# A top-4 mixture-of-experts layer: expert work in 32-token groups on four column tiles, with VectorE turning the rows

## The reference

```python
logits = xt @ w_router + b_router                 # 1024 tokens, 32 experts
top_val, top_idx = lax.top_k(logits, 4)
top_w = softmax(top_val)
...
gate = xblk @ w_gate[e] + b_gate[e]               # per expert, over its tokens
up = xblk @ w_up[e] + b_up[e]
gate = minimum(gate, 7.0); up = clip(up, -7.0, 7.0)
h = (up + 1.0) * gate * sigmoid(1.702 * gate)
y_expert = h @ w_down[e] + b_down[e]
...
y = sum over a token's four experts of top_w * y_expert
out = x + gt2 * rms_norm(y, g_post_ffn)
```

## Time and profile before

| | us |
|---|---|
| median of three runs | 2531.75 |
| the profiled execution, first to last instruction (span) | 2541.4 |
| TensorE busy in it | 2373.6 (93%) |
| VectorE, ScalarE, GpSimd busy | 723.2, 498.1, 421.2 |
| TensorE on the chain that ended last | 88% |
| DMA, mean over the span | 231 GB/s |

### The profile page before, as it was taken

The page is one execution under the profiler, slowest core; times in us unless marked ns, Lnnn a source line. Parts: engine busy times, 40 slices in busy tenths (PEclk is TensorE's granted clock), DMA queues, the critical chain, the costliest instruction groups (busy, mean ns, idle before and its releaser), DMA issues.

```text
span 2541.4 us, 31972 instructions
## 1 busy us (share of the span) xinstructions
PE 2373.6 (93%) x11147; PEld 1211.2 (48%) x11148; DVE 723.2 (28%) x1243; ACT 498.1 (20%) x1116; POOL 421.2 (17%) x528
## 2 busy tenths in 40 slices
PE   5999999998987699999999999999999999999992
PEld 3575756775553354444444444344444444444430
DVE  4155565363466110111111111111111111111114
ACT  5122212233452010111111111111111111111112
POOL 5000000003003631111121111211111111111112
PEclk9999999998986799999999999999999999999996
DMA  8112110136024586677789989889888998999985
GB/s 281 33 34 75 33 46 30 58 99 229 34 93 167 208 283 210 197 269 243 271 298 374 334 293 370 311 311 359 326 277 278 316 330 298 375 328 341 325 310 201
DMA packets 216274, 587.81 MB, mean 231 GB/s; under 512 B 21338, under 2 KB 81266, under 8 KB 216210
## 3 DMA queue, kind: packets, MB, share of 16 engines
q1 hardware_dynamic: 131650, 337.94, 36.1%
q10 hardware_dynamic: 55504, 197.22, 20.7%
q0 software_dynamic: 29056, 51.75, 9.5%
HBM read 548.46 MB, written 38.37 MB: 231 GB/s over the span
## 4 chain that ended last, share of the span: by engine, by line
PE 88%; DVE 4%; issue 2%; DMA 2%; ACT 1%; POOL 1%; ACTq 0%; SPq 0%; DVEq 0%; POOLq 0%
PE ps L1900 25%; PE ps L1927 14%; PE ps L1959 12%; PE ps L1973 7%; PE ps L1656 5%; PE ps L1757 4%; PE ps L1652 4%; PE ps L1662 2%; PE ps L1713 2%; PE ps L1659 2%; PE ps L1938 2%; PE ps L1863 2%; DMA w_up_e<-in_w_up_dram 1%; PE ps L1895 1%; PE ps L1735 1%
## 5 line engine op out<-in xcount | busy, mean ns | idle before, releaser
L1900 PE MATMUL ps<-w_up_e,xT 128*128 128x512 f32 x736 | 345.9, 592 | 0.0
L1900 PE MATMUL ps<-w_gate_e,xT 128*128 128x512 f32 x736 | 345.9, 592 | 0.0
L1959 PE MATMUL ps<-w_down_e,hT 128*128 128x512 f32 x736 | 319.7, 592 | 0.0
L1475 DVE TENSOR_SCALAR oh_gu<-part_e,tab_e 128x128 bf16<-128x128 f32 x48 | 13.8, 287 | 992.2 <-PE ps L1900 598.9
L1030 ACT ACTIVATE sig_sb<-gate_sb 128x1024 f32<-128x1024 f32 x47 | 49.7, 1058 | 1074.4 <-DVE gate_sb L1481 1074.4
L1927 PE MATMUL ps<-w_gate_e,xT 128*32 128x256 f32 (+1 forms) x1504 | 228.4, 473 | 4.2 <-DMA w_up_e<-in_w_up_dram 4.2
L1927 PE MATMUL ps<-w_up_e,xT 128*32 128x256 f32 (+1 forms) x1504 | 227.2, 470 | 0.0
L1900 PEld LDWEIGHTS ps<-w_up_e,xT 128*128 128x128 f32 x736 | 139.8, 190 | 176.0 <-issue 176.0
L1900 PEld LDWEIGHTS ps<-w_gate_e,xT 128*128 128x128 f32 x736 | 139.9, 190 | 168.5 <-issue 165.3
L1959 PEld LDWEIGHTS ps<-w_down_e,hT 128*128 128x128 f32 x736 | 138.0, 190 | 165.0 <-issue 165.0
L1973 PE MATMUL ps<-w_down_e,hT 128*32 128x256 f32 (+1 forms) x1504 | 191.8, 478 | 7.9 <-issue 7.9
(11 more groups left out here) (384 smaller groups left out, 2363.9 us busy)
## 6 DMA issues: line engine op xcount, KB each, us to landing
w_down_e<-in_w_down_dram ACTq DMA_DIRECT2D x368, 512.0 KB, 4.6
w_gate_e<-in_w_gate_dram SPq DMA_DIRECT2D x256, 512.0 KB
w_up_e<-in_w_up_dram SPq DMA_DIRECT2D x256, 512.0 KB
w_ring<-in_w_ada_dram SPq DMA_DIRECT2D x17, 1024.0 KB, 5.2
w_ring<-in_w_in_dram SPq DMA_DIRECT2D x20, 512.0 KB, 5.2
w_first<-in_w_ada_dram SPq DMA_DIRECT2D x7, 1024.0 KB, 12.4
x_all<-in_x_dram SPq DMA_DIRECT2D x2, 2048.0 KB, 10.5
w_out<-in_w_out_dram SPq DMA_DIRECT2D x8, 512.0 KB, 8.6
```

The costliest lines, as they stand in the source:

```text
L1900: last = T.matmul(ps[:, b, :], xT[:, k, :], wgt[b // 2][:, k, (b % 2) * 512:(b % 2) * 512 + 512], start=False, stop=k == KT - 1)
L1959: last = T.matmul(ps[:, 4 + b, :], hT[:, k, :], wgt[2][:, k, b * 512:b * 512 + 512], start=k == 0, stop=k == KT - 1)
```

## The change

The routing, the expert loop and its data layout are rewritten; the mixer is the same.

- **TensorE.** An item is cut into 1 to 4 groups of 32 tokens. For each k-slice and group, four matmuls run on the four column tiles of the array: 32 tokens stand still, tile j streams its quarter of the weight columns, 512 columns for gate and up together, 256 for down. The `rows` and `hidden` transposes, the bias matmuls and `slot_sums` are gone. An item's form is now its number of groups, chosen by nested `If`/`Else`; one register load (`item_pair`) brings the forms of both items and the expert.
- **VectorE.** It turns the gathered rows (`rows_turned`), turns gate and up out of PSUM in 32x32 blocks, adds the bias to the turned values, clamps, multiplies, and writes `hT` directly.
- **GpSimd.** Rows move in quarters (1 KB) so that a group's rows land on four sets of 32 partitions: four gathers and four adding scatters for an item. Each scatter waits until the one before it has landed. `idx_g` and `idx_s` are worked out per item from `slot_tab`.
- **Slots.** A token's slot is (position in its expert, expert) alone, so VectorE's `place(t)` and GpSimd's `put_slots(t)` run tile by tile beside the routing; SyncE reads the finished table back by four DMAs.

The core of the diff (removed and added):

```diff
-            with pe.Fori(0, n_before) as i:
-                v_down = item_variant(pe, i)
-                rows(i + 2)
-                down(i, v_down)
-                e, v = item_expert(pe, i + 2), item_variant(pe, i + 2)
-                gate_up(i + 2, e, v)
+            def gate_up_of(m, loaded, n):
+                for k in range(KT):
+                    pe.wait_ge(gu_in[k], loaded)
+                    for g in range(n):
+                        if k == 0 and g == 2 and not (isinstance(m, int) and m < 1):
+                            pe.wait_ge(gu_evac, m * 2)
+                            apart(pe)
+                        for j in range(4):
+                            last = T.matmul(
+                                ps[j * GROUP:(j + 1) * GROUP, g, :].rearrange("p (w b f) -> p w b f", w=2, f=GROUP),
+                                xT[:, k, g * GROUP:(g + 1) * GROUP],
+                                w_gu[:, :, k, :].rearrange("p w (b q f) -> p w b q f", q=4, f=GROUP)[:, :, :, j, :],
+                                start=k == 0, stop=k == KT - 1)
+                    last.then_inc(gu_used, 1)
...
+            def down_of(m, n):
+                for k in range(KT):
+                    pe.wait_ge(dn_in[k], m * 16 + 16)
+                    for g in range(n):
+                        for j in range(4):
+                            last = T.matmul(
+                                ps[j * GROUP:(j + 1) * GROUP, 4 + g // 2, g % 2 * QUARTER:(g % 2 + 1) * QUARTER],
+                                hT[:, g, k, :], w_dn[:, k, j * QUARTER:(j + 1) * QUARTER],
+                                start=k == 0 and g % 2 == 0, stop=k == KT - 1, skip_group_check=True)
+                    last.then_inc(d_used, 1)
...
+            with pe.Fori(0, n_before) as i:
+                pair = item_pair(pe, i)
+                down(i, pair & 3)
+                gate_up(i + 2, (pair >> 4) * 32, (pair >> 2) & 3)
```

```diff
+            def scatter(m, g):
+                pool.wait_ge(y_added, m * (16 * GROUPS) + 16 * (Y_ZERO + g))
+                apart(pool)
+                G.indirect_dma_start(y_quarters, bass.IndirectOffsetOnAxis(ap=idx_s[:, g:g + 1].bitcast(U32), axis=0),
+                                     yrow[:, g, :], None, compute_op=ALU.add).then_inc(y_added, 16)
...
             with pool.Fori(0, n_before) as i:
-                scatter(i)
-                next_gather(i + 4)
+                gather_begun(i + 4)
+                scatter_begun(i)
+                for g in range(GROUPS):
+                    scatter(i, g)
+                    gather(g)
```

```diff
+                for half in range(2):
+                    V.transpose(guT[:, 2 * half:2 * half + 2].rearrange("p g w b i -> p (g w b i)"),
+                                ps[:, 2 * half:2 * half + 2, :].rearrange("p a n -> p (a n)")).then_inc(gu_evac, 1)
+                dve.wait_ge(gu_evac, m * 2 + 2)
...
+                lk(V.tensor_tensor(both, both, biasT[:, :, bass.ds(e, 1)].unsqueeze(1).to_broadcast(
+                    [P, GROUPS, 2 * KT, GROUP]), ALU.add))
+                V.tensor_scalar(g, g, SWIGLU_LIMIT, None, ALU.min).then_inc(gate_ready, 1)
+                lk(V.tensor_scalar(u, u, SWIGLU_LIMIT, -SWIGLU_LIMIT, ALU.min, ALU.max))
...
+            def rows_turned(m):
+                dve.wait_ge(xg_in, m * (16 * GROUPS) + 16 * GROUPS)
+                if not (isinstance(m, int) and m < 1):
+                    dve.wait_ge(xT_ready, m)
+                V.transpose(xr[:].rearrange("p g b i -> p (g b i)"), xg[:].rearrange("p g c -> p (g c)")
+                            ).then_inc(xr_ready, 1)
```

More of the change, by code:

```diff
@@ L155, in hybrid_block_kernel @@
+        w_dn = region(72, 104)("w_down_e", KT, D)
         y_all = region(0, 32)("y_all", TL, D)
[L156 to L165, removed]
@@ L1293, in _ @@
             gate_head(HEADS - 1)
+            for b in range(4):
+                for q in range(4):
+                    last = V.tensor_copy(fm_q[b * GROUP:(b + 1) * GROUP, :, 2 * q:2 * q + 2],
+                                         fm[q * GROUP:(q + 1) * GROUP, :, b:KT:4])
+            last.then_inc(fm_ready, 1)
             dve.wait_ge(proj_evac, len(units))
@@ L1331, in weigh @@
-                last.then_inc(w_full_ready, 1)
-                dve.wait_ge(w_full_ready, t + 1)
-                rest = w_full
-                for piece in range(3):
-                    part = rtab_bf[:, t, 3 + piece * NE:3 + (piece + 1) * NE]
-                    link(V.tensor_copy(part, rest[:, t, :]))
-                    if piece < 2:
-                        link(V.tensor_tensor(rtab[:, t, :], rest[:, t, :], part, ALU.subtract))
-                        rest = rtab
-            dve.wait_ge(pieces, 1)
@@ L1529, in _ @@
[L1529 to L1538 removed]
+                if not (isinstance(m, int) and m < 1):
+                    dve.wait_ge(hT_ready, m)
+                dve.wait_ge(gu_used, m * KT + KT)
@@ L1932, in hidden @@
-            def hidden(m):
-                pe.wait_ge(h_ready, m + 1)
-                pe.wait_ge(xT_ready, m + 2)
-                apart(pe)
-                for k in range(KT):
-                    last = T.transpose(ps[:, 6 + k // 4, (k % 4) * P:(k % 4 + 1) * P], h_sb[:, k * P:(k + 1) * P],
-                                       ident[:])
-                last.then_inc(hT_psum, 1)
-            def down(m, v=None):
+            T.matmul(ps[:, 0, TAB_AT:TAB_AT + 3 * NTAB], ones[:], tab_diag[:].rearrange("p a n -> p (a n)"),
+                     start=True, stop=True).then_inc(tab_psum, 1)
@@ new lines, in _, with gate_up @@
+            for t in range(2, 4):
+                first_rows(t)
+            weights_turned(4, 4)
+            for t in range(4, TL):
+                first_rows(t)
+            def gate_up(m, loaded, size):
+                pe.wait_ge(xT_ready, m + 1)
+                if not (isinstance(m, int) and m < 1):
+                    pe.wait_ge(gu_evac, m * 2 - 1)
+                apart(pe)
+                with pe.If(size == 3):
+                    gate_up_of(m, loaded, 4)
+                with pe.Else():
+                    with pe.If(size == 2):
+                        gate_up_of(m, loaded, 3)
+                    with pe.Else():
+                        with pe.If(size == 1):
+                            gate_up_of(m, loaded, 2)
+                        with pe.Else():
+                            gate_up_of(m, loaded, 1)
@@ L1943, in down @@
+            def down(m, size):
                 pe.wait_ge(hT_ready, m + 1)
@@ L1979, in _ @@
-            first_rows(1)
-            pe.wait_ge(tables, 1)
-            second = item_second(pe, 0)
-            pe.wait_ge(pieces, 1)
-            pe.wait_ge(weighed, 1)
-            slot_sums(0, second)
-            weights_turned(4, 4)
-            for t in range(2, 4):
-                first_rows(t)
-            n_last = last_item(pe)
-            e, v = item_expert(pe, 0), item_variant(pe, 0)
-            slot_sums(1)
-            pe.wait_ge(wT_ready, TL)
-            rows(0)
-            first_rows(4)
```

821 lines of the change are left out of this document (271 added, 550 removed).

## The result

The changed kernel takes 3439.43 us (median of four runs, 3434.93 to 3443.25) where the kernel before takes 2531.69: a ratio of 1.357, 95% interval 1.355 to 1.360. It is slower, as forecast, but by 908 us and not by 454, and outside the range. The loop made it so: up to 798 us of the profiled execution TensorE is busy for 731.7 us where it was for 726.9.

The account below looks back on a forecast made before the run. TensorE was taken as the bound. The 2541 us span with -122 work, +15 tile form, +553 instruction fetch, -5 start and +15 tail gave 2997, stated as 2985 us; range 2460 to 3200, the case's own 2650 to 3200.

Parts of the forecast that it names:

- 2,600 instructions are too much to keep: TensorE's loop body: 10.4 transfers of code, assumed not kept, so each of 45 turns fetches what it jumps to.
- the two signs for the skips: Before TensorE's projections: one-group forms idling long and four-group forms little would confirm that skipped code costs by distance.
- TensorE's work: Expert loop: transposes and biases go, 2.6 us for each of 47 items, -122 us; column-tile form adds +15.
- Weights: Expert loop: weights late by 114 us at most, about 50 showing if nothing else slowed TensorE; nothing with the fetches.
- Rival A: TensorE's loop code: all 10.4 transfers stay kept, so no fetch cost; -47, 2485 us (2440 to 2540), chance 0.26.
- the price of instruction fetch: TensorE's loop: 3.6 transfers waited for per turn at 2.8 us, plus low clock, over 45 turns: +553 us.
- 2.2 us for the low clock: TensorE's loop: matmuls behind a stop run slower, 5.87 us instead of 3.66, counted once in each of 45 turns.
- start -5, tail +15: Kernel's ends: tables made beside the routing save 5 us; the last item's serial scatters and shuffles add 15.
- Rival C: Whole kernel: one 2.8 us fetch a turn (+126) cancels the transposes' gain; 2527 to 2537 us, chance 0.03.
- the serial scatters: GpSimd's queue: four scatters, each behind the last one's landing, hidden under a 44 us turn; 0, at most +115.
- Rival B: GpSimd's serial scatters bind through yrow, with code kept, at steps over 6.6 us; about 2650 us, chance 0.09.
- the sentence on the gathers of item i+4: GpSimd's queue: these gathers stand behind a waiting scatter but are due only two items later; hidden, 0.

Follow-up runs that it names:

- e11: e1 plus 32 matmuls (128 instructions) that never run in the loop's body, 1,720 instructions in all: 2570.3 us, 45 q8 transfers.
- e7: e1 plus 64 matmuls (256 instructions) that never run in the loop's body, 1,850 instructions in all: 3178.2 us, 442 q8 transfers.
- e1: Changed kernel with TensorE's four forms of each projection replaced by two shared steps (groups 2 and 3, then 0 and 1), about 1,590 instructions: 2561.89 us, ratio 1.008.
- e6: e5 with an item's four scatters issued without waiting for one another, padding rows separate for each group: 2467.28 us, ratio 0.973 to the kernel before.
- e9: Changed kernel plus 320 matmuls (1,280 instructions, five blocks) that never run, in front of down's forms: 3647.23 us, +208.
- e4: Kernel before the change plus 320 matmuls (1,280 instructions) that never run in its loop's body: 3313.17 us, +774, 487 q8 transfers.
- e10: Changed kernel with the chain of conditions choosing a form turned into a balanced two-level tree in both projections: 3343.41 us, -96.
- e5: e1 with GpSimd's four gathers of item i+4 issued before the serial scatters of item i, no longer between them: 2517.71 us, ratio 0.994.

## Why the prediction was right in its mechanism and wrong in its size

**What held.** TensorE was the bound of the loop before, busy for 1554.24 of 1576 us at a granted clock of 1.00. That 2,600 instructions are too much to keep was an assumption, which no row showed; e11 and e7 put the limit between 1,720 and 1,850. Nor does a row show where q8 brings the code from: the page has 548.73 MB read from HBM in e1 and in the changed kernel alike, with 45 and 539 transfers on q8. The order of events: q8 returned to the loop, the idle time stands on "issue" in front of down and of gate and up, the granted clock is under 0.9 (0.846), and nothing in the loop waits for weights. q8 came out above the 150 to 500 transfers of the text (539), and a turn's idle time at 18.8 us where some 10 were put. Of the two signs for the skips, forms of one group do wait long (20.3 to 21.0 us in the rows above), but forms of four wait for 2.4 to 12.3, which the count by distance does not give. TensorE's work fell by 105 us where -122 + 15 was put (e1 against before). Weights: 54 us of waits in e6, 50 in the text. Rival A, "the code stays", is in effect e6 with its 2467 against 2485; with the scatters as the change has them it is e1, 2562, outside A's 2440 to 2540. The column tiles cost next to nothing: in e6 down and gate and up of a whole item take 13.81 and 27.47 us from start to start, and took 13.74 and 27.47.

**The step that failed** is the price of instruction fetch, "3.6 that is waited for, x 2.8 = 10.1 us, and 2.2 us for the low clock: 12.3 x 45 = +553". Measured: idle time on issue in front of the loop's two groups 883 us against some 36 in the loop of before, +847 or 18.8 us a turn; low clock +154, 3.4 us a turn; together +1001. That is 1001 us where 553 were put, and the step fails in its count of fetches waited for, in the price and in the clock:

- *The unit.* I counted blocks skipped by distance (0, 2, 3.5 or 4.5 for the four forms). e9 shows that distance is not what is paid for: five blocks stepped over cost 4.8 us, as in the row of e4, and e10 that fewer jumps over the same distance cost less. What counts is taken branches into code that isn't there: the jump back, 0.94 from condition to condition on the way to a form in each projection (0, 1, 2 or 3 for 23, 9, 10 and 5 items), and one over the remaining forms behind each long form (32 of 47): 1 + 1.9 + 1.4 = 4.3 a turn. The count of 3.6 was near this by chance.
- *The price.* 2.8 us came from the first turn, all stops divided by all transfers. But the short stops there (1.02 to 2.49) lie between transposes that follow each other straight on, and the dear ones (4.77 and 9.00) behind the conditions. By jumps the mean is 18.8/4.3 = 4.4 us; e9 gives 4.8 with two transfers, e10 3.2 with one. The row was read with the wrong divisor.
- *The clock.* I took one slow start in a turn; there are two, since gate and up stop again after down. Only where four groups of gate and up followed a down of one or two did the second start come without a stop (27.68 us for the gate and up at 1198.01, where those behind a stop took 29.0 to 30.5).

The remaining terms (start -5, tail +15) come out of the balance at about -4 together and decide nothing.

Two sums of the text don't add up, and neither enters the forecast. Rival C by its own terms (-122 + 15 + 126 + 15 - 5) is +29, or 2560 us, not 2527 to 2537. And the serial scatters are put at "at most +115 (below)", where the text below has 160 over A.

**The range.** The bounds in the text went from +126 to +1310 us for this term, but the case's own range ended at 3200, +770. The upper end of a range has to stand where the bound puts it as long as no row excludes that; the text only had an argument (code run straight on comes in time), which holds (the 256 records of four groups of gate and up run in 29.37 us without a stop among them), but for the wrong unit.

**Rival B** was true and hidden. In e1 scatters mostly stand 7 to 10 us apart, above the 6.6 from which it was to decide, and serial scatters with gathers between them cost about 95 us, not the 160 of the text. Nearly half of that came through a link that B did not price: the sentence on the gathers of item i+4, which stand behind a waiting scatter, ends at 0, and e5 shows some 40 us for their place once the long turns don't cover it.

## What to carry to other kernels

Count a loop body's instructions before writing out one more form: here a body of 1,720 instructions was kept and one of 1,850 was not (e11, e7), and the step between them was 608 us in 45 turns. If it has to be larger, then count the taken branches in a turn, not the code: by themselves they cost 2.4 to 4.8 us each in the rows above, 4.4 in the mean, and two in quick succession more than their sum. Replacing chains of conditions by a balanced tree gave 96 us back here and hinting the jump back 82; the two were not run together. Putting the most frequent form where no jump leads to it follows from the count, but no run tests it. Build forms from shared parts (groups 2 and 3, then 0 and 1) where that keeps the body small, and look for q8 inside the loop and for idle time on "issue" when an engine with nothing to wait for stands still.

## What the runs showed that was not expected

- Code that never runs is not free: 128 instructions more (e11 to e7) cost 608 us.
- A jump over five blocks that are not held cost 4.8 us and brought two transfers (e9); jumps between forms one or two blocks apart cost 3.2 and brought one (e10).
- The loss by a low clock after stops is under a fifth of the loss by the stops themselves: 154 us to 847.
- A scatter's landing came later where more else moved. In e1, where the DMA engines are busy for 0.85 of the loop, a step of issue and landing is 8 to 10 us in the item shown, though steps of 4.6 occur in its loop too; in the changed kernel's quiet end (0.29 between 3370 and 3400 us) four scatters follow each other at 4.6 us. What lengthens a landing was not tested. Three of the four:

```profile
3379.59 1.55 POOL L658 DMA_INDIRECT y_rows<-yrow,idx_s  x1 [0.94 <-POOL idx_s L632]
3384.11 1.55 POOL L658 DMA_INDIRECT y_rows<-yrow,idx_s  x1 [2.96 <-DMA y_rows<-yrow,idx_s]
3388.74 1.55 POOL L658 DMA_INDIRECT y_rows<-yrow,idx_s  x1 [3.09 <-DMA y_rows<-yrow,idx_s]
```
